# Gathered expert rows for 40 tokens instead of 32, in an encoder block with 16384 product-key experts

## The chip, the core and the metric

The kernel is written by hand in instructions with semaphores and runs on one core of one Trainium2 chip. The metric is the device time of one launch in microseconds (us), as the median of several runs. One core has TensorE (PE; its weight loads are told apart as PEld), VectorE (DVE), ScalarE (ACT), GpSimd (POOL) and SyncE (SP, here only a queue that issues DMAs). "L1014" is line 1014 of the kernel.

## What is computed

One block over 256 tokens of width 2048 (`SEQ`, `D_MODEL`), all in float32. Norm, one large projection, two attention branches, gates, output projection, residual: this part takes the first 700 us and isn't touched. Then comes the expert layer, in the reference:

```python
def peer_ffn(h, w_pq, sub_keys, expert_u, expert_v):
    ...
    q = (t @ w_pq).reshape(n_tok, PEER_HEADS, 2, PEER_QDIM // 2)
    sc = jnp.einsum('thcd,hckd->thck', q, sub_keys, preferred_element_type=jnp.float32)
    top_s, top_i = lax.top_k(sc, PEER_TOPK)
    ...
    best_s, best_j = lax.top_k(cand_s, PEER_TOPK)
    expert_idx = jnp.take_along_axis(cand_i, best_j, axis=-1)
    gate = jax.nn.softmax(best_s, axis=-1)
    ...
        u = expert_u[ib]
        a = jax.nn.gelu(jnp.einsum('thkd,td->thk', u, tb, preferred_element_type=jnp.float32), approximate=False)
        vv = expert_v[ib]
        return jnp.einsum('thk,thkd->td', (gb * a).astype(vv.dtype), vv)
```

Each token picks 8 x 16 = 128 of the 16384 experts. For each it takes the dot of its own 2048 values with the expert's row of `expert_u`, a gelu, a gate, and adds the expert's row of `expert_v` with that weight. A last residual and a norm follow.

## The kernel before

**Two ways to the experts.** The first TD = 224 tokens go through all 16384 experts on TensorE, with a weight that is zero where an expert isn't picked. The last S = 32 tokens fetch only the rows that they picked, by gathers; VectorE multiplies them. S + TD = 256.

**Chunks.** All weights stream in as chunks of 128 x 1024 floats (512 KB), through four buffers (`raw`). ACT rounds a chunk to `hi` (L622), DVE takes the rest `lo` = raw - hi (L1014, two buffers). PE multiplies `hi` with the activations' high and low part side by side ("high" matmul, 2 x TD columns, L1643 in stage "u", L1912 in "down") and `lo` with the high part ("low" matmul, TD columns, L1650 and L1916). A body is four chunks; each has 8 highs and 8 lows. In chunks 0 and 2 of a body the highs come first, in 1 and 3 the lows, so on PE 16 of a kind stand in a row.

**Stage "u"** has 256 chunks (bodies 0 to 63): h times expert_u, gelu, into `act`. In bodies 1 to 21 DVE also finds the picked experts. At body 20 two matmuls with a selection matrix (`sel`, L1872 and L1873) put the picked indices and gates of the last 32 tokens on partitions: four copies (COPIES) of 32 tokens, each copy with another quarter of the 128 picks, so 32 gathers (PICKS) of 128 rows cover the half rows of one table, and STEPS = 64 both halves. In bodies 24 (U0) to 51 (UG - 1) the gates of the dense tokens are **spread** over all experts, four pairs of tokens a body, 112 pairs: POOL writes two `one_j` tiles a pair (L602, four buffers), DVE one `one_i` (L1479, two buffers), PE multiplies them before chunks 0 and 2 of a body, two pairs at a time (L1896, two records each matmul), ACT copies one part of the result (L909), DVE multiplies the other into `act` (L1489). Of each later block DVE multiplies gelu and gate itself (L1499).

**Dots.** POOL issues the gathers (L583) from its own queue, in an order written out with its one_j: the gather of row n + 2 before pair 4n + 2. DVE's dot (L1453) reads the row, which then is free for the next gather but one (two row buffers). `dots_of` (L144) puts one dot after chunk 3 of each body from 22 (UR) to 51, then two a body; the last is in body 4 of "down".

**Stage "down"** has two halves of 128 chunks (32 bodies): act times expert_v, for output columns 0 to 1023 and 1024 to 2047. ACT and DVE make `act_now` (L924, L1531) for each chunk. In the first half, after body WEIGHED = 5, DVE adds the gathered rows of expert_v, weighted, into `acc` (L1563, L1566); `adds_of` (L151) puts one in every 2.75 chunks of the first half, from chunk 28 on, and one in every 3.5 of the second. In the last body of each half PE adds the copies up by a product with `fold` (L1968), after it has waited for all adds of that half.

**Queues.** Each engine runs its instructions in the order in which the kernel gives them. SP's queue holds all loads of weights in order; a load waits until `lo` of the chunk four before is made. Each engine's order in a body is that of its functions: DVE in the spread does lo of the next chunk, one_i, the sum of the block's two halves (`upper`, L1020, chunks 0 and 2), act x gates, act x upper (chunks 1 and 3), and the dot last.

## Time and profile before

| | |
|---|---|
| time, median of 3 runs (range) | 2140.78 us (2140.64 to 2142.12) |
| profiled execution, its time | 2139.2 us |
| its span, first to last instruction | 2137.2 us |
| PE busy | 2108.7 us, 99% |
| DVE busy | 1584.1 us, 74% |
| ACT busy | 1118.9 us, 52% |
| POOL busy | 488.8 us, 23% |
| DMA | 482.26 MB, mean 226 GB/s |

The page counts an engine as busy while an instruction of it runs, and matmuls overlap, so a busy PE is not one at its peak; how fast it goes is read from the starts in the timeline. Shares of busy time are means over stages with different limits. Stage "u" lies between 772.8 and 1469 us, its spread between 1010 and 1345, "down" between 1470 and 2123.

### The profile page before, as it was taken

The numbers are of one execution on the slowest core, as the hardware profiler recorded it, in microseconds if no ns is written. First come the engines' busy times: TensorE is split into PE (matmuls) and PEld (weight loads), VectorE is DVE, ScalarE is ACT, GpSimd is POOL, SyncE is SP. The second block draws the span as 40 slices with busy tenths as digits, with TensorE's granted clock in tenths as the row PEclk, the third lists the DMA queues.
The fourth block names the chain that finished last, engine by engine and source line by source line (L and its number), as shares of the span: only waits on it lengthen the run. The fifth ranks groups of instructions, "written<-read, shape, count | busy, mean of one in ns | idle before, by whom it ended". The sixth has DMA issues, their size and how long they took to land.

```text
span 2137.2 us, 40878 instructions
## 1 busy us (share of the span) xinstructions
PE 2108.7 (99%) x13494; PEld 1973.4 (92%) x13494; DVE 1584.1 (74%) x2622; ACT 1118.9 (52%) x1879; POOL 488.8 (23%) x379
## 2 busy tenths in 40 slices
PE   8999999999999999999999999999999999999997
PEld 6888888889989999999999999999999999999997
DVE  6555566667777986888778888888777776777775
ACT  5444455446455655556555555555555554555553
POOL 0000000000000000001999999332222220111110
PEclk9999999999999999999999999999999999999998
DMA  7655554445556556666767666888877776877773
GB/s 246 235 187 190 183 166 157 149 155 189 181 192 230 166 174 210 207 210 224 228 221 222 222 221 222 286 309 313 312 286 291 285 283 215 267 275 266 268 251 128
DMA packets 134750, 482.26 MB, mean 226 GB/s; under 512 B 15455, under 2 KB 18399, under 8 KB 134295
## 3 DMA queue, kind: packets, MB, share of 16 engines
q1 hardware_dynamic: 116072, 414.29, 57.6%
q0 software_dynamic: 18432, 67.12, 8.8%
q8 instruction: 27, 0.44, 0.1%
q14 instruction: 45, 0.36, 0.1%
q10 hardware_dynamic: 174, 0.05, 0.0%
HBM read 477.16 MB, written 4.24 MB: 225 GB/s over the span
## 4 chain that ended last, share of the span: by engine, by line
PE 95%; DVE 3%; issue 1%; DMA 1%; ACT 0%; DVEq 0%; SPq 0%; ACTq 0%
PE ps L1643 35%; PE ps L1912 19%; PE ps L1650 19%; PE ps L1916 11%; PE ps L1673 5%; PE ps L1896 2%; DVE lo L1014 1%; PE ps L1767 1%; PE ps L1749 1%; PE ps L1758 0%; DMA raw<-w_down 0%; DMA x_t<-x_t 0%; DVE score_b L1322 0%; DVE idx_now L1324 0%; DVE top_now L1328 0%
## 5 line engine op out<-in xcount | busy, mean ns | idle before, releaser
L1014 DVE TENSOR_TENSOR lo<-raw,hi 128x1024 fp32r<-128x1024 f32 x760 | 935.3, 1231 | 473.5 <-PE ps L1643 144.5
L622 ACT CAST hi<-raw 128x1024 fp32r<-128x1024 f32 x760 | 795.7, 1053 | 346.8 <-DMA raw<-w_down 137.6
L1643 PE MATMUL ps<-move_u,hi 128*128 128x448 f32 x2048 | 451.1, 368 | 0.0
L1912 PE MATMUL ps<-act_now,hi 128*128 128x448 f32 x2048 | 439.8, 365 | 0.4 <-ACT hi L622 0.4
L1912 PEld LDWEIGHTS ps<-act_now,hi 128*128 128x128 f32 x2048 | 375.0, 188 | 26.4 <-issue 0.7
L1643 PEld LDWEIGHTS ps<-move_u,hi 128*128 128x128 f32 x2048 | 371.0, 189 | 24.6
L1643 PE MATMUL ps<-move,hi 128*128 128x512 f32 x1536 | 379.3, 395 | 9.5 <-ACT hi L622 9.5
L1643 PEld LDWEIGHTS ps<-move,hi 128*128 128x128 f32 x1536 | 281.5, 189 | 62.9 <-issue 9.5
L630 ACT COPY upper<-ps 128x224 f32<-128x224 f32 (+1 forms) x224 | 80.3, 358 | 484.3 <-PE ps L1643 484.2
L602 POOL TENSOR_SCALAR one_j<-iota,j_t,gate_t 128x128 f32<-128x128 f32 x224 | 296.8, 1331 | 3.0 <-ACT j_t L880 1.8
L1916 PEld LDWEIGHTS ps<-act_now,lo 128*128 128x128 f32 x2048 | 250.6, 191 | 7.3 <-DVE lo L1014 2.0
L1916 PE MATMUL ps<-act_now,lo 128*128 128x224 f32 x2048 | 252.1, 274 | 2.1 <-DVE lo L1014 2.0
L1650 PEld LDWEIGHTS ps<-move_u,lo 128*128 128x128 f32 x2048 | 248.4, 191 | 5.1 <-DVE lo L1014 1.5
L1650 PE MATMUL ps<-move_u,lo 128*128 128x224 f32 x2048 | 249.0, 274 | 1.1 <-DVE lo L1014 1.0
L1650 PEld LDWEIGHTS ps<-move,lo 128*128 128x128 f32 x1536 | 198.1, 191 | 11.2 <-DVE move L1066 1.3
L1650 PE MATMUL ps<-move,lo 128*128 128x256 f32 x1536 | 202.3, 284 | 1.0 <-DVE move L1239 0.9
L583 POOL DMA_INDIRECT rows<-w_down,idx x64 | 93.9, 1467 | 452.5 <-DVE acc L1566 371.7
L583 POOL DMA_INDIRECT rows<-u_rows,idx x64 | 85.8, 1341 | 437.8 <-ACT gates_s L866 318.2
L1531 DVE TENSOR_TENSOR act_now<-act,act_now 128x224 fp32r<-128x224 f32 x256 | 98.8, 386 | 13.3 <-ACT act_now L924 12.9
L1673 PE MATMUL ps<-move,hi 128*128 128x256 f32 x512 | 97.4, 286 | 2.8 <-DVE lo L1014 2.8
L924 ACT CAST act_now<-act 128x224 fp32r (+1 forms) x256 | 95.7, 374 | 0.0
L554 POOL COPY q_now<-qk 128x256 f32 x8 | 4.1, 515 | 363.5 <-DVE qk L1027 207.0
(206 smaller groups left out, 1628.2 us busy)
## 6 DMA issues: line engine op xcount, KB each, us to landing
raw<-w_u SPq DMA_DIRECT2D x256, 512.0 KB
raw<-w_down SPq DMA_DIRECT2D x256, 512.0 KB
raw<-w_qk SPq DMA_DIRECT2D x68, 512.0 KB
raw<-w_gate SPq DMA_DIRECT2D x64, 512.0 KB
raw<-w_out SPq DMA_DIRECT2D x32, 512.0 KB
raw<-w_pq SPq DMA_DIRECT2D x32, 512.0 KB
raw<-w_v SPq DMA_DIRECT2D x28, 512.0 KB
raw<-w_o SPq DMA_DIRECT2D x24, 512.0 KB
```

The source lines that it names most:

```text
L583: nc.gpsimd.indirect_dma_start(rows[n % 2][:], None, lines, bass.IndirectOffsetOnAxis(ap=idx[:, n:n + 1], axis=0)).then_inc(row_landed[n % ...
L602: ins = nc.gpsimd.tensor_scalar(one_j[n % 4][:, t % 2, :], iota128[:], j_t[:, t:t + 1], gate_t[:, t:t + 1], ALU.is_equal, ALU.mult)
L622: nc.scalar.copy(hi[slot][:], raw[slot][:]).then_inc(hi_ready, 1)
L630: nc.scalar.copy(upper[e][:, 0:w], ps[e][:, w:2 * w]).then_inc(upper_ready, 1)
L924: nc.scalar.copy(act_now[s % ACTS][:, 0:TD], pick1(act, j)).then_inc(act_hi_ready, 1)
L1014: nc.vector.tensor_tensor(lo[s % LOS][:], raw[s % RAW][:], hi[s % RAW][:].bitcast(F32), ALU.subtract).then_inc(lo_ready, 1)
L1531: nc.vector.tensor_tensor(act_now[s % ACTS][:, TD:2 * TD], pick1(act, j), act_now[s % ACTS][:, 0:TD].bitcast(F32), ALU.subtract).then_inc( ...
L1643: ins = nc.tensor.matmul(ps[bank][:, 0:2 * w], hi[slot][:, col:col + P], m, start=begins, stop=ends)
L1650: ins = nc.tensor.matmul(ps[bank][:, 0:w], lo[lslot][:, col:col + P], m[:, 0:w], start=False, stop=False, skip_group_check=True)
L1673: ins = nc.tensor.matmul(ps[bank][:, 0:T], w[:, col:col + P], x, start=begins, stop=ends)
L1912: return nc.tensor.matmul(ps[d][:, 0:2 * TD], hi[s % RAW][:, d * P:(d + 1) * P], act_now[s % ACTS][:], start=begins, stop=ends)
L1916: return nc.tensor.matmul(ps[d][:, 0:TD], lo[s % LOS][:, d * P:(d + 1) * P], act_now[s % ACTS][:, 0:TD], start=False, stop=False, skip_gro ...
```

## The change

S becomes 40 and TD 216; 40 tokens in three copies fill 120 partitions (NP). A copy has a third of the picks, so PICKS is 43 in place of 32 and STEPS 86 in place of 64. PAIRS is 108 (was 112) and the spread ends after body 50. There are three row buffers (ROWS) instead of two. DOT_AT, a list, holds the place of each dot: after chunk 3 of every body from 22, after chunk 1 too in the odd bodies 25 to 49 and in all from 51 on; the last is in body 8 of "down" and WEIGHED is 9. In the spread, the gather of a row now stands before the pair two places ahead of its dot. The adds start at chunk 44 of "down" and come every 1.88 chunks in the first half, from chunk 2 of the second every 2.88; the last of each half is at its chunk 123. Gathers of expert_v no longer wait for all dots, only for their own buffer. The selection is six matmuls with three matrices, the indices are copied by two ACT instructions in place of eight. `fold` is loaded before x2, when PE is through with stage "u".

```diff
-S = 32
+S = 40
 TD = T - S
 COPIES = P // S
-PICKS = PH * TOPK // COPIES
+NP = COPIES * S
+PICKS = -(-PH * TOPK // COPIES)
+ROWS = 3
 STEPS = 2 * PICKS
...
+DOT_AT = [it * BODY + s for it in range(UR, (CHUNKS["u"] + CHUNKS["down"]) // BODY) for s in (1, 3)
+          if s == 3 or it >= UG or it > U0 and it % 2 != U0 % 2][:STEPS]
+WEIGHED = DOT_AT[-1] // BODY + 1 - CHUNKS["u"] // BODY
...
+def row_before_pair(n):
+
+    return tuple(g for g in range(2, STEPS) if DOT_AT[g] < UG * BODY and max(0, DOT_AT[g] - U0 * BODY - 2) == n)
...
-    first, apart = (2, 7 / 2) if half else ((WEIGHED + 2) * BODY, 11 / 4)
+    first = 2 if half else (WEIGHED + 2) * BODY
+    apart = (HALF * BODY - 5 - first) / (PICKS - 1)
...
             sp.wait_ge(move_free, 1)
+            sp.dma_start(fold[:], A["fold"]).then_inc(fold_in, 16)
...
-                if table == "u_rows" and n >= 2:
-                    pool.wait_ge(dot_done, n - 1)
-                if table == "w_down":
-                    pool.wait_ge(dot_done, min(STEPS, STEPS - 1 + n))
-                    if n >= 2:
-                        pool.wait_ge(row_added, n - 1)
+                g = n + STEPS * (table == "w_down")
+                if ROWS <= g:
+                    pool.wait_ge(dot_done, min(STEPS, g - ROWS + 1))
+                if ROWS + STEPS <= g:
+                    pool.wait_ge(row_added, g - ROWS - STEPS + 1)
...
             for n in range(PAIRS):
-                if n % BODY == 2:
-                    gather("u_rows", n // BODY + 2)
+                for g in row_before_pair(n):
+                    gather("u_rows", g)
...
-                    for q in range(COPIES):
-                        own = slice(q * S, (q + 1) * S)
-                        nc.scalar.copy(idx[own, :].rearrange("p (c m) -> p c m", c=2),
-                                       ps[7][own, 0:2 * P].rearrange("p (c k) -> p c k", c=2)[:, :, own])
-                        ins = nc.scalar.copy(gates_s[own, :], ps[7][own, 2 * P + q * S:2 * P + (q + 1) * S])
-                    ins.then_inc(idx_ready, 1)
+                    nc.scalar.copy(idx[0:NP, :], ps[7][0:NP, 0:STEPS])
+                    nc.scalar.copy(gates_s[0:NP, :], ps[7][0:NP, 2 * P:2 * P + PICKS]).then_inc(idx_ready, 1)
...
+            for q, own in enumerate(own_of):
+                nc.tensor.matmul(chosen[:, :, 0:own.stop - own.start], sel[:, q, :], e_pair[:, :, own],
+                                 start=q == 0, stop=q == COPIES - 1)
+            for q, own in enumerate(own_of):
+                ins = nc.tensor.matmul(ps[7][0:NP, 2 * P:2 * P + own.stop - own.start], sel[:, q, :], found_g[:, 1, own],
+                                       start=q == 0, stop=q == COPIES - 1)
...
                 pe.wait_ge(row_added, PICKS * (half + 1))
+                pe.wait_ge(fold_in, 16)
```

## Rows read from the trace of the kernel before

**Rows 1.** The page: engines busy, and the chain that ended last by engine.
```profile
PE 2108.7 (99%) x13494; PEld 1973.4 (92%) x13494; DVE 1584.1 (74%) x2622; ACT 1118.9 (52%) x1879; POOL 488.8 (23%) x379
...
PE 95%; DVE 3%; issue 1%; DMA 1%; ACT 0%; DVEq 0%; SPq 0%; ACTq 0%
```
**Rows 2.** Timeline of PE, stage "qk": start us, duration us, instructions.
```profile
102.73 3.82 PE L1643 MATMUL ps<-move,hi 128*128 128x512 f32 x16
106.39 2.08 PE L1650 MATMUL ps<-move,lo 128*128 128x256 f32 x16
108.30 3.82 PE L1643 MATMUL ps<-move,hi 128*128 128x512 f32 x16
```
**Rows 3.** Timeline of PE, stage "u" before the spread.
```profile
902.18 1.94 PE L1650 MATMUL ps<-move_u,lo 128*128 128x224 f32 x16
903.96 3.40 PE L1643 MATMUL ps<-move_u,hi 128*128 128x448 f32 x16
907.20 1.94 PE L1650 MATMUL ps<-move_u,lo 128*128 128x224 f32 x16
```
**Rows 4.** Timeline of PE, the fold matmuls and what follows them.
```profile
1785.22 1.88 PE L1968 MATMUL ps<-fold,acc 128*128 128x32 f32 x16
...
1786.93 1.13 PE L1916 MATMUL ps<-act_now,lo 128*128 128x224 f32 x8
```
**Rows 5.** Timeline of PE in the spread.
```profile
1206.82 1.05 PE L1896 MATMUL ps<-one_j,one_i 128*128 128x128 f32 x8
...
1212.74 1.05 PE L1896 MATMUL ps<-one_j,one_i 128*128 128x128 f32 x8
```
**Rows 6.** Timeline of POOL in the spread.
```profile
1204.00 1.03 POOL L583 DMA_INDIRECT rows<-u_rows,idx  x1 [0.17 <-issue]
1205.07 10.60 POOL L602 TENSOR_SCALAR one_j<-iota,j_t,gate_t 128x128 f32<-128x128 f32 x8
```
**Rows 7.** Line L602: durations ns (least, median, most), idle before them.
```profile
L602 POOL TENSOR_SCALAR one_j<-iota,j_t,gate_t x224: 783/1401/3615, 1009.6 to 1340.3; 128x128 f32<-128x128 f32 x112
...
  ACT j_t L880: 1.8, 1
```
**Rows 8.** Timeline of POOL at the spread's end.
```profile
1335.31 5.73 POOL L602 TENSOR_SCALAR one_j<-iota,j_t,gate_t 128x128 f32<-128x128 f32 x4
```
**Rows 9.** Timeline of all engines there: PE's last spread.
```profile
1342.98 1.05 PE L1896 MATMUL ps<-one_j,one_i 128*128 128x128 f32 x8
```
**Rows 10.** Timeline of POOL, one narrow window: a single one_j.
```profile
1206.56 3.01 POOL L602 TENSOR_SCALAR one_j<-iota,j_t,gate_t 128x128 f32<-128x128 f32 x1
```
**Rows 11.** Timeline of DVE in the same stretch.
```profile
1206.71 1.22 DVE L1453 CUSTOM_DVE_ANT_0 rows<-rows,h_rows 128x1024 f32<-128x1024 f32 x1
...
1208.99 0.42 DVE L1479 TENSOR_TENSOR one_i<-ps,iota 128x256 f32<-128x256 f32 x1
```
**Rows 12.** Stretches of POOL: from:to, us, busy (instructions), PEclk, DMA share, GB/s.
```profile
1027.47:1033.37 5.90, 5.90 (x4) 1.00 0.78 220
1033.38:1038.06 4.68, 4.68 (x4) 1.00 0.66 197
1205.07:1211.12 6.05, 6.05 (x4) 1.00 0.73 212
1211.14:1215.66 4.52, 4.52 (x4) 1.00 0.65 205
```
**Rows 13.** Timeline of POOL late in stage "u".
```profile
1429.92 1.68 POOL L583 DMA_INDIRECT rows<-u_rows,idx  x1 [3.34 <-DVE dots L1453]
```
**Rows 14.** Timeline of DVE late in the spread.
```profile
1322.96 1.33 DVE L1014 TENSOR_TENSOR lo<-raw,hi 128x1024 fp32r<-128x1024 f32 x1 [1.08 <-ACT hi L622]
...
1328.88 1.23 DVE L1014 TENSOR_TENSOR lo<-raw,hi 128x1024 fp32r<-128x1024 f32 x1
```
**Rows 15.** Line L1566: durations ns of the adds.
```profile
L1566 DVE SCALAR_TENSOR_TENSOR acc<-rows,w_s,acc x62: 1276/1279/1280, 1548.2 to 2073.4; 128x1024 f32<-128x1024 f32 x62
```
**Rows 16.** Stretches of all engines: busy PE, PEld, DVE, ACT, POOL, then as above.
```profile
1380.00:1420.16 40.16, 40.16 (x257) 38.33 (x257) 33.24 (x49) 22.27 (x33) 13.41 (x9) 1.00 0.89 318
```

More of the change, by code:

```diff
@@ L366, in build @@
         e_pair = at("e_pair", ARENA + 98 * KB, [P, 2, P])
-        sel = at("sel", ARENA + 99 * KB, [P, P])
-        rows = [at(f"rows{i}", ARENA + (112 + 4 * i) * KB, [P, CW]) for i in range(2)]
+        sel = at("sel", ARENA + 96 * KB, [P, COPIES, NP])
+        rows = [at(f"rows{i}", ARENA + (112, 116, 108)[i] * KB, [P, CW]) for i in range(ROWS)]
         acc = at("acc", ARENA + 120 * KB, [P, D])
         idx = at("idx", MOVE + 31 * KB, [P, STEPS], U32)
-        dots = at("dots", MOVE + 31 * KB + 256, [P, STEPS])
-        gates_s = at("gates_s", MOVE + 31 * KB + 512, [P, PICKS])
-        w_s = at("w_s", MOVE + 31 * KB + 640, [P, PICKS])
-        fold = at("fold", MOVE + 31 * KB + 768, [P, S])
+        dots = at("dots", MOVE + 31 * KB + 352, [P, STEPS])
+        gates_s = at("gates_s", MOVE + 31 * KB + 704, [P, PICKS])
+        w_s = dots[0:NP, 0:PICKS]
+        fold = at("fold", MOVE + 16 * KB + 2 * TD * 4, [P, S])
         x2 = at("x2", MOVE, [P, KT, T])
@@ L606, in _ @@
             nc.gpsimd.memset(ones[:], 1.0).then_inc(ones_ready, 1)
-            for n in range(PAIRS // BODY + 2, STEPS):
-                gather("u_rows", n)
+            for n in range(STEPS):
+                if DOT_AT[n] >= UG * BODY:
+                    gather("u_rows", n)
             for n in range(STEPS):
@@ L1449, in dot_of @@
             def dot_of(n):
-                v.wait_ge(row_landed[n % 2], 16 * (n // 2 + 1))
-                c = n // PICKS * CW
-                nc.vector.tensor_tensor_reduce(rows[n % 2][:], rows[n % 2][:], h_rows[:, c:c + CW], 1.0, 0.0, ALU.mult, ALU.add,
-                                               dots[:, n:n + 1]).then_inc(dot_done, 1)
+                v.wait_ge(row_landed[n % ROWS], 16 * (n // ROWS + 1))
+                c, row = n // PICKS * CW, rows[n % ROWS][0:NP, :]
+                nc.vector.tensor_tensor_reduce(row, row, h_rows[0:NP, c:c + CW], 1.0, 0.0, ALU.mult, ALU.add,
+                                               dots[0:NP, n:n + 1]).then_inc(dot_done, 1)
             def dots_at(it, s):
@@ L1549, in weights_at @@
                     v.wait_ge(dot_done, STEPS)
-                    nc.vector.tensor_tensor(w_s[:], dots[:, 0:PICKS], dots[:, PICKS:STEPS], ALU.add).then_inc(w_summed, 1)
+                    nc.vector.tensor_tensor(w_s, dots[0:NP, 0:PICKS], dots[0:NP, PICKS:STEPS], ALU.add).then_inc(w_summed, 1)
                 if (it, s) == (WEIGHED + 1, 1):
@@ L1870, in _ @@
             pe.wait_ge(e_ready, 1)
-            pe.wait_ge(sel_in, 16 * 2)
-            nc.tensor.matmul(ps[7][:, 0:2 * P], sel[:], e_pair[:].rearrange("p c k -> p (c k)"), start=True, stop=True)
-            nc.tensor.matmul(ps[7][:, 2 * P:3 * P], sel[:], found_g[:, 1, :], start=True, stop=True).then_inc(e_turned, 1)
+            pe.wait_ge(sel_in, 16)
+            own_of = [slice(q * PICKS, min((q + 1) * PICKS, P)) for q in range(COPIES)]
+            chosen = ps[7][0:NP, 0:2 * PICKS].rearrange("p (c m) -> p c m", c=2)
+            for q, own in enumerate(own_of):
[4 more added lines that the diff above has]
+                                       start=q == 0, stop=q == COPIES - 1)
+            ins.then_inc(e_turned, 1)
             with pe.Fori(INDEXED, UR + 1) as it:
@@ L1905, in _ @@
                     body("u", two * 2 + (U0 + k), before=spread_gates(k))
+            for it in range(UG - (UG - U0) % 2, UG):
+                body("u", it, before=spread_gates((it - U0) % 2))
             with pe.Fori(UG, CHUNKS["u"] // BODY) as it:
@@ L1966, in last_body @@
                 pe.wait_ge(row_added, PICKS * (half + 1))
+                pe.wait_ge(fold_in, 16)
                 for d in range(8):
-                    nc.tensor.matmul(ps[d][:, 2 * TD:2 * TD + S], acc[:, (8 * half + d) * P:(8 * half + d + 1) * P], fold[:],
+                    nc.tensor.matmul(ps[d][:, 2 * TD:2 * TD + S], acc[0:NP, (8 * half + d) * P:(8 * half + d + 1) * P], fold[0:NP, :],
                                      start=False, stop=False, skip_group_check=True)
@@ L2038, in columns, with own_copies @@
     return np.ascontiguousarray(b.reshape(-1, P, CW))
+def own_copies():
+    sel = np.zeros((P, COPIES, NP), np.float32)
+    for q in range(COPIES):
+        sel[P - S:, q, q * S:(q + 1) * S] = np.eye(S, dtype=np.float32)
+    return sel
 def weave(wa, wb):
@@ L2061 @@
         "ident": np.eye(P, dtype=np.float32),
-        "sel": np.ascontiguousarray(np.tile(np.eye(P, dtype=np.float32)[:, P - S:], (1, COPIES))),
-        "fold": np.tile(np.eye(S, dtype=np.float32), (COPIES, 1)),
+        "sel": own_copies(),
+        "fold": np.pad(np.tile(np.eye(S, dtype=np.float32), (COPIES, 1)), ((0, P - NP), (0, 0))),
         "bias_rows": bias_rows(),
```

36 lines of the change are left out of this document (17 added, 19 removed).

## The prediction

> **What bounds the kernel now.** I read the page first: PE is busy for 99% of the span and holds 95% of the chain that ended last [rows 1]. So time goes down only if TensorE has less to stream, and goes up wherever another engine makes it wait. What it streams follows from the code: eight "high" matmuls of 448 columns and eight "low" ones of 224 for each of the 512 chunks of the expert layer, 4096 of either kind. The timeline of PE then gives the pitch of each kind, start to start, which the mean duration hides because matmuls overlap: 16 highs of 512 columns take 106.39 - 102.73 = 3.66 us, 16 of 448 take 3.24 us; 16 lows of 256 columns take 1.91 us, of 224 take 1.78 us [rows 2, 3]; 16 matmuls of only 32 columns take 1.71 us [rows 4]. Last I looked at who runs beside PE while the gates are spread (1010 to 1345 us), because there POOL is busy all the time.
>
> **TensorE, what is removed.** TD goes from 224 to 216, so a high has 432 columns. From 512 to 448, 64 columns fewer save 0.42 us per 16, so 16 fewer save 0.105 us; 4096/16 = 256 such groups give 26.9 us. All of it lies on the path, as PE is it. For the lows (224 to 216) I take nothing: the pitch at 224 columns is 111 ns and at 32 columns still 107 ns, so what sets it is no longer columns. The bounds are 0 and, by the slope between 256 and 224 columns (0.13 us per 16 for 32), 0.13/4 x 256 = 8.3 us.
>
> Here a rule of the Trainium skill speaks for more: "TensorE: Matmul & The Clock Gate", section "Back-to-back issue gap", has an isolated gap of N/2.4 + 2.5 ns, by which 4096 lows would give 4096 x 8/2.4 ns = 13.7 us more (an estimate from that page). The trace contradicts it at these widths, with 107 ns at 32 columns, and the page itself says that the formula undercounts at small N.
>
> **Smaller parts on PE.** There are 108 pairs of tokens to spread in place of 112. Two pairs (8 records) lengthen a half body from 5.02 us [rows 3] to 5.92 us [rows 5], so a pair costs 0.45 us: 1.8 us saved. Picking the gathered indices takes six matmuls in place of two; a float32 matmul leaves two records, as those of the spread do, so it is eight records more at some 0.11 us: 0.9 us lost. The fold matmuls have 40 columns in place of 32, at the same floor [rows 4]: nothing. **Without any new wait PE saves 26.9 + 1.8 - 0.9 = 27.8 us.**
>
> **POOL in the spread, where a wait is added.** This is the part that decides. For each pair POOL writes two one_j tiles, and a body holds four pairs. In steady state its timeline is one gather (1.03 us), gaps of 0.17 and 0.04 us, and eight one_j in 10.60 us: 11.84 us, which is exactly twice PE's 5.92 [rows 5, 6]. It never waits for a buffer to come free: the only idle time before any of the 224 one_j is 1.8 us at the very start, and none of them waits for a matmul of the spread [rows 7]. An engine with time to spare would run ahead to its four buffers and wait there. This one stays about 2 us ahead of its need to the end: the last one_j ends at 1341.04, the last two pairs are multiplied from 1342.98, the second of them 0.45 us later, 2.4 us after [rows 8, 9]. So POOL has no surplus.
>
> Why it is so slow: a one_j takes 783 ns when free and up to 3615 [rows 7]. The one of 1206.56 takes 3.01 us: meanwhile DVE runs the dot (from 1206.71) and the next lo, both with two inputs in SBUF, and it ends 0.58 us after that lo has given way to one_i at 1208.99, which has one input in PSUM [rows 10, 11]. So a dot on DVE costs POOL time, too. Four one_j in a half with a dot take 5.90 us early and 6.05 in the middle; in a half without, 4.68 and 4.52 [rows 12]. The difference is 1.22 to 1.53 us, about one dot (1.22 us [rows 11]).
>
> The Trainium skill has the rule behind this ("SBUF — State Buffer", section "Who interferes with whom"): a DVE instruction with two SBUF inputs contends with a GpSimd instruction that reads SBUF, and the second to come blocks. The trace agrees. It speaks against this change.
>
> The change puts three gathers and three dots where two bodies had two of each, and it does so 13 times (bodies 25 to 49). Per two bodies POOL gets 1.03 + 0.17 + 0.04 = 1.24 us more of gather and 1.22 to 1.53 of waiting, and the time that PE leaves it shrinks by 4 x 0.105 = 0.42 us. In full that is 2.88 to 3.19 us. If the gather falls into a wait that POOL has anyway it costs nothing: 1.22 + 0.42 = 1.64 us. The new gathers stand between the two pairs of a half, mostly after the long wait and not in it, but a late POOL shifts them; gathers of the later stage wait themselves (1.68 us in place of 1.03) [rows 13]. Below 1.64 only a finer interlocking of the two engines could bring it: the end is 0. I take a third of the gather, 2.05 us: 13 x 2.05 = 26.7 us, less the 2.4 us of lead that POOL has once: **24.3 us**. Queued behind POOL are only its own one_j and gathers; PE waits for the one_j at the spread's matmuls, and everything else waits for PE.
>
> **DVE.** A half body with a dot is full late in the spread: lo at 1322.96, the next released lo at 1328.88, no idle, 5.92 us; the half without ends with 1.08 us idle [rows 14]. In 5.82 us a half with a dot overruns by at most 0.10, three in a row by 0.3, and the fourth gives back over 1. DVE makes a lo while PE is still in the chunk before, which hides it: nothing; without that cover it would be 39 x 0.1 = 3.9 us. In "u" after body 51 a pair of chunks has one dot as now. In "down" the dots go on to body 8 in place of 4 and the adds come every 1.88 chunks in place of 2.75 and every 2.88 in place of 3.5. An add is 1.28 us [rows 15]: per 4.91 us DVE has two lo (2.46 [rows 14]), two act_now (some 0.8, estimated from the 0.42 of one_i over 256 columns [rows 11]) and 1.06 adds (1.36), together 4.62. It fits; the five places where adds follow in neighbouring chunks overrun for one pair: 0 to 2 us, I take 0.
>
> **DMA.** A gather moves 0.49 MB. With a chunk (0.524 MB) every 2.46 us, the dot phase has the same 313 GB/s as now, and the adds of the first half 213 + 106 = 320 GB/s. Now 318 GB/s, at a DMA share of 0.89, leave PE without a gap (40.16 us busy of 40.16) [rows 16]. Cost 0, and up to 3 us if 320 is just too much. SP issues one small load (fold) more before x2, while four chunks are in flight: nothing. The last add is at chunk 123 of 128, PE asks for it after chunk 124, 2.5 us later; its cover is thin but it happens only twice: 0 to 2 us, I take 0. Three row buffers give each gather one more dot of time to land; PE waits for no row now, so nothing is gained. The eight small ACT copies that become two are beside PE.
>
> **The sum.** The profiled execution took 2139.2 us, 1.6 below the median of 2140.78. From the median: 2140.8 - 27.8 + 24.3 = **2137 us**.
>
> **The rivals.** (a) POOL interlocks with DVE as well with three dots as with two, and the columns are gained in full: 2140.8 - 27.8 = 2113, with small remains 2110 to 2122. For it: the lead of 2.4 us has been constant, so the present rate is a locked one and need not be the highest. Against it: no time is left over and the demand grows by a tenth. 24%. (b) The lows shrink with their columns after all, by the slope between 256 and 224: 8 us less than the forecast, 2129, or 2105 together with (a). Against it: the 107 ns at 32 columns. 6%. (c) Slower: the new gather falls outside the waits each time, so that POOL is short by the full 2.88 to 3.19 us per two bodies; 13 times that less 2.4 is 35 to 39 us, and the time 2148 to 2152. It decides from (27.8 + 2.4)/13 = 2.32 us per two bodies on; from 2.65 on it can be measured. For it: order of the gathers. 14%. (d) That the change doesn't do what it says: DVE or DMA hold up the down stage by 3 to 5 us; inside the range of the forecast.
>
> **How the numbers follow.** The forecast has 56%, and its own range is 2131 to 2145 (1.64 us to some 2.7 per two bodies). A measurement here tells about 0.2% (4.3 us) from no change: faster means below 2136.5, slower above 2145. Of the forecast's 56, 24 lie below, 30 within, 2 above. With (a) and (b) faster has 54%, within 30%, slower 2 + 14 = 16%. The range takes in (a) and reaches to the beginning of (c): 2110 to 2149; what it leaves out is most of (c) and what is worse.
>
> **What would show it.** Right: PE at 432 columns has 16 highs in about 3.14 us and 16 lows still in 1.78; POOL busy without a gap from the first to the last one_j; the spread's matmuls wait for one_j, mostly in odd bodies; 27 bodies of the spread take more than 27 x 11.63 = 314 us, some 338. Under (a) they take 314 and no wait for POOL is in the list. Under (b) the lows have a pitch of 109 ns. Wrong in kind: idle time of PE in the dot or add phases, with DMA or DVE as its releaser.

## The result, and the profile after

The changed kernel takes 2200.56 us (median of 4 runs, 2195.37 to 2206.2), the kernel before 2141.45 beside it (2140.64 to 2145.96): ratio 1.0272, 95% interval 1.0242 to 1.0302. It is slower by 59 us where 4 us less were forecast, and lies above the whole range. The profiled run took 2199.36 us, with a span of 2197.6. Ratios here and below are those of executions side by side, so they differ a little from the quotients of the medians, and one slow execution of e1 (2288.26 us at a mean granted clock of 0.849, where its nine others have 0.993 to 0.996) is left out of its ratio.

From the page of the changed kernel: PE's row, the DMA share in 40 slices, the two big DMA queues (packets, MB, share of 16 engines), the chain by engine and by line.

```profile
PE 2109.4 (96%) x13486; PEld 1986.5 (90%) x13486; DVE 1635.3 (74%) x2680; ACT 1114.6 (51%) x1867; POOL 532.9 (24%) x415
...
DMA  7655554445556567668777778999999998999994
...
DMA packets 141087, 499.84 MB, mean 227 GB/s; under 512 B 17534, under 2 KB 20478, under 8 KB 140630
...
q1 hardware_dynamic: 116072, 414.41, 59.0%
q0 software_dynamic: 24768, 84.56, 15.0%
...
PE 61%; DMA 13%; POOL 13%; DVE 7%; issue 3%; ACT 1%; SPq 0%; DVEq 0%; ACTq 0%; POOLq 0%
```

Before, PE held 95% of the chain and DMA 1% [rows 1]; now 61%, with DMA and POOL at 13% each. From the kernel before, the same two queues, and one stretch of 100 us (busy PE, PEld, DVE, ACT, POOL, then granted clock, DMA share, GB/s):

```profile
q1 hardware_dynamic: 116072, 414.29, 57.6%
q0 software_dynamic: 18432, 67.12, 8.8%
...
1500.00:1600.00 100.00, 100.00 (x637) 95.33 (x636) 75.84 (x102) 54.93 (x84) 20.11 (x13) 1.00 0.83 300
```

q0 carries the gathered rows. Its bytes grew by a quarter, its share of the engines by 70%. The number that decides this case is the engine time of one gathered row, small packets included: share x span x 16 / rows. Before it is 0.088 x 2137.2 x 16 / (128 gathers x 128 rows) = 184 ns, after it is 0.150 x 2197.6 x 16 / (172 x 120) = 256 ns.

Where the time went is read from the starts of the matmuls in PE's timeline: first matmul of "u", first and last of the spread, first, middle and last "high" of down (us), in the profiled execution of each kernel. e1 and e5 are two of the experiments below. "PE alone" marks the shortest that any kernel here with 432 columns had.

```
stage                before   changed   e1     e5     PE alone
u before the spread  244.6    240.5     240.6  240.5  240.5
spread               326.4    336.4     332.3  322.1  309.2
u after it           126.1    147.5     133.7  133.4  133.4
down, first half     325.5    359.9     321.6  321.1  321.1
down, second half    327.4    325.0     326.6  325.3  323.8
span                 2137.2   2197.6    2144.0 2131.1
```

The spread grew as forecast, though it has one body less (27 for 28; that body now counts in the stage after it, which at PE's own pace would take 133.4 us for 126.1). Over "PE alone" the two stages behind the spread are 14.1 and 38.8 us too long, and for those the forecast had nothing. Stretches of the changed kernel there, with the same columns:

```profile
1400.00:1470.00 70.00, 64.00 (x392) 60.14 (x391) 50.66 (x74) 31.80 (x48) 17.25 (x13) 0.98 1.02 282
1500.00:1600.00 100.00, 91.49 (x562) 87.08 (x563) 73.61 (x108) 47.32 (x74) 27.84 (x18) 0.97 1.02 294
1700.00:1830.00 130.00, 117.22 (x745) 111.67 (x743) 97.98 (x117) 59.69 (x92) 32.82 (x24) 1.00 1.02 280
```

The DMA engines are full (1.02) and move only 282, 294 and 280 GB/s; before they moved 318 at 0.89 [rows 16]. Before, PE was busy in all of the 100 us from 1500, with 300 GB/s at 0.83. The waits of the changed kernel name the same, and POOL's one_j in the spread (us in total, times, longest):

```profile
ACT hi L631 <- DMA raw<-w_down: 309.0, 191, 5.1
...
ACT hi L631 <- DMA raw<-w_u: 60.4, 45, 2.8
...
PE ps L1932 <- DVE lo L1019: 30.7, 33, 2.5
...
PE ps L1910 <- POOL one_j L610: 17.8, 9, 3.4
```

The chunk (raw) lands late, ACT's hi and DVE's lo with it, and PE waits for lo: the list shows DVE, the cause is one step further back, at the DMA. PE's wait is the one that counts: before, it was 2.0 us at this place and not 30.7. ACT's wait for raw alone tells little, as it is 276.8 us in e1 below too, where PE waits for lo 4.0 us.

Some of PE's stalls cost more than themselves, as the granted clock falls with them. Before, it was 1.00 in every stage from the spread to the end of down; here it is 0.98 over the spread, and 0.97 or 0.98 in two of the stretches above. One case in the spread, from PE's timeline, and the stretch from 1040.3 us (busy PE, PEld, DVE, ACT, POOL, then as above):

```profile
1041.30 1.22 PE L1910 MATMUL ps<-one_j,one_i 128*128 128x128 f32 x4 [3.04 <-POOL one_j L610]
1042.16 3.23 PE L1650 MATMUL ps<-move_u,hi 128*128 128x432 f32 x8
1045.19 2.87 PE L1657 MATMUL ps<-move_u,lo 128*128 128x216 f32 x16
1047.89 1.75 PE L1650 MATMUL ps<-move_u,hi 128*128 128x432 f32 x8
...
1040.30:1047.10 6.80, 5.80 (x22) 5.57 (x22) 0.32 (x2) 1.73 (x4) 6.49 (x8) 0.50 0.68 183
```

PE waits 3.04 us, and from 1040.3 to 1047.1 us the granted clock is 0.50 (1.2 GHz): eight highs then take 3.03 us and the sixteen lows 2.70, where they take 1.66 and 1.77 at 1.00. A share of 0.98 over 336 us means some 13 us at that level, an estimate, so up to some 6 of the spread's 27 us over "PE alone" are the clock. The forecast had no such term.

PE's own pitch at the full clock is what was forecast, in its timeline:

```profile
1604.97 3.31 PE L1928 MATMUL ps<-act_now,hi 128*128 128x432 f32 x16
1608.12 1.94 PE L1932 MATMUL ps<-act_now,lo 128*128 128x216 f32 x16
1609.89 2.32 PE L1928 MATMUL ps<-act_now,hi 128*128 128x432 f32 x11
```

Sixteen highs take 1608.12 - 1604.97 = 3.15 us (3.24 at 448 columns), sixteen lows 1609.89 - 1608.12 = 1.77 [rows 3].

### The profile page after: what moved, and what is told of

Read it like the earlier page. It is cut to its first block, busy times and chain, and to the rows that moved or that the text cites. A ratio compares the mean times of both kernels' runs of the same rounds, so it can differ in the third digit from the quotient of the medians.

```text
span 2197.6 us, 40971 instructions
## 1 busy us (share of the span) xinstructions
PE 2109.4 (96%) x13486; PEld 1986.5 (90%) x13486; DVE 1635.3 (74%) x2680; ACT 1114.6 (51%) x1867; POOL 532.9 (24%) x415
## 4 chain that ended last, share of the span: by engine, by line
PE 61%; DMA 13%; POOL 13%; DVE 7%; issue 3%; ACT 1%; SPq 0%; DVEq 0%; ACTq 0%; POOLq 0%
PE ps L1650 24%; PE ps L1657 13%; POOL one_j L610 11%; PE ps L1928 11%; DMA raw<-w_down 9%; PE ps L1932 6%; PE ps L1680 5%; DVE lo L1019 4%; DMA raw<-w_u 4%; POOL rows L591 2%; PE ps L1756 1%; PE ps L1774 1%; ACT hi L631 1%; DMA raw<-w_o 0%; PE ps L1765 0%
## 5 line engine op out<-in xcount | busy, mean ns | idle before, releaser
L1650 PE MATMUL ps<-move_u,hi 128*128 128x432 f32 x2048 | 442.8, 364 | 0.1
L1928 PE MATMUL ps<-act_now,hi 128*128 128x432 f32 x2048 | 433.6, 362 | 3.8 <-DVE act_now L1536 1.6
L639 ACT COPY upper<-ps 128x216 f32<-128x216 f32 (+1 forms) x224 | 79.1, 353 | 460.4 <-PE ps L1650 458.7
L1932 PE MATMUL ps<-act_now,lo 128*128 128x216 f32 x2048 | 258.2, 275 | 30.7 <-DVE lo L1019 30.7
L1657 PE MATMUL ps<-move_u,lo 128*128 128x216 f32 x2048 | 255.2, 277 | 9.6 <-DVE lo L1019 9.5
L591 POOL DMA_INDIRECT rows<-u_rows,idx x86 | 119.4, 1388 | 491.8 <-ACT gates_s L872 313.8
L591 POOL DMA_INDIRECT rows<-w_down,idx x86 | 123.4, 1435 | 438.2 <-DVE acc L1573 372.5
L1536 DVE TENSOR_TENSOR act_now<-act,act_now 128x216 fp32r<-128x216 f32 x256 | 96.9, 379 | 90.3 <-ACT act_now L929 88.1
L1573 DVE SCALAR_TENSOR_TENSOR acc<-rows,dots,acc 120x1024 f32<-120x1024 f32 x84 | 107.4, 1279 | 0.0
L1458 DVE CUSTOM_DVE_ANT_0 rows<-rows,h_rows 120x1024 f32<-120x1024 f32 x86 | 105.3, 1225 | 0.0
```

The lines of the kernel that those rows point to most:

```text
L591: nc.gpsimd.indirect_dma_start(rows[g % ROWS][0:NP, :], None, lines, bass.IndirectOffsetOnAxis(ap=idx[0:NP, n:n + 1], axis=0)).then_inc(ro ...
L1458: nc.vector.tensor_tensor_reduce(row, row, h_rows[0:NP, c:c + CW], 1.0, 0.0, ALU.mult, ALU.add, dots[0:NP, n:n + 1]).then_inc(dot_done, 1)
L1536: nc.vector.tensor_tensor(act_now[s % ACTS][:, TD:2 * TD], pick1(act, j), act_now[s % ACTS][:, 0:TD].bitcast(F32), ALU.subtract).then_inc( ...
L1573: nc.vector.scalar_tensor_tensor(out=own, in0=row, scalar=w_s[:, m:m + 1], in1=own, op0=ALU.mult, op1=ALU.add).then_inc(row_added, 1)
L1650: ins = nc.tensor.matmul(ps[bank][:, 0:2 * w], hi[slot][:, col:col + P], m, start=begins, stop=ends)
L1657: ins = nc.tensor.matmul(ps[bank][:, 0:w], lo[lslot][:, col:col + P], m[:, 0:w], start=False, stop=False, skip_group_check=True)
```

## The experiments

My theory after the result: 120 rows in one gather are dear for the DMA, whatever the amount. Rival: it is the amount, a quarter more rows in the densest stretch. Four kernels separate them.

**e1: 128 rows, the rest as changed.** The index tile, the gather and `sel` get all 128 partitions, the last eight with rows that nobody reads.

```diff
+GP = P
...
-                nc.gpsimd.indirect_dma_start(rows[g % ROWS][0:NP, :], None, lines,
-                                             bass.IndirectOffsetOnAxis(ap=idx[0:NP, n:n + 1], axis=0)
+                nc.gpsimd.indirect_dma_start(rows[g % ROWS][0:GP, :], None, lines,
+                                             bass.IndirectOffsetOnAxis(ap=idx[0:GP, n:n + 1], axis=0)
```

> The changed kernel, but each gather fetches 128 rows: the selection has 128 columns in place of 120, so the eight added partitions get index 0 and fetch a row that nobody uses. Theory A (a gather of 120 rows is split badly over the DMA engines: after shows 253 ns per gathered 4 KB against 182, and 24 small packets per gather against 16): packets fall back to 16 small ones per gather and some 185 ns per row although 6.7% more bytes move; the DMA share in the dot and add phases falls from 1.0 to about 0.9, PE's gaps there go, and the time falls from 2200 by 50 to 62 us to 2138 to 2150. What remains above 2114 is POOL's part. Rival B (what saturates is the amount: 86 x 2 gathers with three buffers): 6.7% more bytes make it slower or leave it as it is, 2195 to 2215.

Measured: 2147.15 us, ratio 1.0018 (1.0007 to 1.0029). Its two queues, and two stretches:

```profile
q1 hardware_dynamic: 116072, 414.42, 58.3%
q0 software_dynamic: 24768, 90.19, 11.8%
...
1400.00:1470.00 70.00, 70.00 (x456) 68.29 (x455) 58.56 (x86) 39.47 (x57) 24.25 (x14) 1.00 0.91 324
1500.00:1600.00 100.00, 98.82 (x640) 96.03 (x639) 79.44 (x115) 53.39 (x83) 27.70 (x17) 1.00 0.89 315
```

More bytes in the same number of packets, and 0.118 x 2144.0 x 16 / (172 x 128) = 184 ns per row, as before the change. 1.0272 - 1.0018 = 0.0254, or 54 us (some 7 either way by the two intervals): that is the price of 120 rows. It takes in what they do to the weights, whose packets are as many and as large in both kernels and took 0.583 x 2144.0 = 1250 us of each engine here, but 0.590 x 2197.6 = 1297 beside the gathers of 120 rows. Amount as the cause falls: 324 GB/s pass with PE busy all the time.

**e2 and e3: the kernel before with 120 and 112 rows** per gather (the results of the last 8 and 16 partitions are left out). The edit of the gather for 120 rows is shown; dots and adds are narrowed in the same way.

```diff
-                nc.gpsimd.indirect_dma_start(rows[n % 2][:], None, lines,
-                                             bass.IndirectOffsetOnAxis(ap=idx[:, n:n + 1], axis=0)
+                nc.gpsimd.indirect_dma_start(rows[n % 2][0:120, :], None, lines,
+                                             bass.IndirectOffsetOnAxis(ap=idx[0:120, n:n + 1], axis=0)
```

> The kernel before (32 tokens, two row buffers), but gathers, dots and adds run over 120 of the 128 partitions; the results of eight partitions (tokens 24 to 31 of the last copy) are left out. Fewer bytes move than before. Theory A: gathered rows take about 255 ns in place of 182, 24 small packets per gather, the DMA share at 1400 to 1450 us rises from 0.9 to about 1.0 and the kernel becomes slower than before by 5 to 30 us. Rival B (amount): 0 to 2 us faster or unchanged.

> The same with 112 rows, of which the results of 16 partitions are left out. If what matters is that the number of rows divides by 16 (16 x 7), it is like before: 16 small packets per gather, about 180 ns a row, time within 3 us of before. If anything but 128 is slow, the rows take about 255 ns and it is slower by 5 to 30 us as with 120.

Measured: 2162.31 us with 120 rows (1.0089, 1.0069 to 1.0109), 2146.06 with 112 (1.0021, 1.0007 to 1.0035). In e2, with one stretch, then e3:

```profile
DMA packets 134750, 478.07 MB, mean 222 GB/s; under 512 B 16479, under 2 KB 19423, under 8 KB 134295
...
q0 software_dynamic: 18432, 62.93, 11.1%
...
1400.00:1470.00 70.00, 63.53 (x378) 58.76 (x379) 50.10 (x74) 33.33 (x48) 20.93 (x13) 0.98 0.98 267
```
```profile
q0 software_dynamic: 16384, 58.73, 8.8%
```

120 rows cost 19 us even in the old kernel, with less to move; from 1400 to 1470 us PE is busy for 63.53 us in place of 69.64, with the DMA at 0.98. A row takes 249 ns there, 210 ns at 112, where the kernel loses 4.5 us (1.5 to 7.5). The packets show how a gather is made up: 18432 / 128 = 144 = 120 rows + 24 small packets; at 112 rows 128 = 112 + 16.

**e4: the changed kernel without second dots in the spread**, so 13 gathers more fall behind it.

```diff
-          if s == 3 or it >= UG or it > U0 and it % 2 != U0 % 2][:STEPS]
+          if s == 3 or it >= UG][:STEPS]
```

> The changed kernel without the second dot in odd bodies of the spread: DOT_AT has those 13 dots and gathers later, so the dots end some 6 bodies later in down and the adds of the first half come closer together. My theory of POOL: its stalls in the spread (27 us of excess against 53 half bodies of 5.82 us) go to 0 to 5 us. The 13 gathers move into the phases in which DMA is full, where each costs its transfer, some 1.5 to 2 us: 20 to 26 us lost there. Sum 2190 to 2205. Rival: if the spread is as long as before without the second dot (337 us from its first to its last matmul), POOL isn't stalled by dot and gather but by something else.

Measured: 2219.48 us (1.0356, 1.0331 to 1.0380). The spread is 309.2 us, which is 53 half bodies of 5.82 us and 0.8 for the last pairs, and no wait for one_j is left: with one dot per body POOL costs nothing even at 432 columns. But the first half of down grows from 359.9 to 398.6:

```profile
1700.00:1830.00 130.00, 100.79 (x572) 93.67 (x573) 87.57 (x100) 47.55 (x72) 42.17 (x30) 0.92 1.03 256
```

27 us won where POOL was the limit were lost, and 16 more, where the DMA is: 43 us in all, where I had expected to lose 20 to 26. Part of it is the clock, 0.92 in the stretch shown. So the second dots are right in kind; what is left of them in e1, 23.1 us of spread, is POOL's price.

**e5 and e6: POOL's price, two ways down**, both with 128 rows. e5 issues each gather of the spread one pair earlier, between the halves of a body and not between the two pairs whose one_j one half waits for. e6 puts the second dot in every fourth body.

```diff
-    return tuple(g for g in range(2, STEPS) if DOT_AT[g] < UG * BODY and max(0, DOT_AT[g] - U0 * BODY - 2) == n)
+    return tuple(g for g in range(2, STEPS) if DOT_AT[g] < UG * BODY and max(0, DOT_AT[g] - U0 * BODY - 3) == n)
```
```diff
-          if s == 3 or it >= UG or it > U0 and it % 2 != U0 % 2][:STEPS]
+          if s == 3 or it >= UG or it > U0 and it % 4 == (U0 + 1) % 4][:STEPS]
```

> The changed kernel with gathers of 128 rows, and each row gather of the spread issued one pair earlier, so that GpSimd does it between the two halves of a body and not between the two pairs whose one_j one half waits for. If the order inside the body is what makes GpSimd hold TensorE back in the spread (332.3 us from its first to its last matmul with 128 rows, floor 309.3), a good part of the 23 us goes: spread 315 to 325, time 2132 to 2140. If GpSimd's work per body is simply too long (8 one_j of 1.30, two gathers and the time it is blocked by dots against 11.64 us of TensorE), the order changes nothing: spread 332, time 2147.

> The changed kernel with gathers of 128 rows and the second dot of the spread in every fourth body in place of every second, so half of the 13 extra dots and gathers move out of the spread into the last stretch of u and the first of down. By GpSimd's price per extra gather and dot the spread comes down from 332.3 us by half of its 23 us excess, to about 321. Theory: with gathers of 128 rows the DMA has room late, so the last stretch of u and the first half of down lengthen by no more than 3 us and the time is 2134 to 2140, below both kernels. Rival: the DMA takes it back as it did without any second dots (152.3 and 398.6 us with 120 rows): then these two stretches lengthen by over 10 us and the time is 2145 to 2160.

Measured: e5 2133.72 us, ratio 0.9964 (0.9949 to 0.9980); e6 2134.73, ratio 0.9964 (0.9953 to 0.9976). Both beat both kernels, the one before by 0.4%, which is little but outside the intervals. Spread 322.1 and 320.6 us, first half of down 321.1 and 325.2. Why the order helps is to be seen in POOL's own rows; durations (least, median, most) of the gathers and the one_j from 1020 to 1320 us, and PE's wait for one_j in the whole run, first e1, then e5:

```profile
L592 POOL DMA_INDIRECT rows<-u_rows,idx x36: 1026/1027/2098, 1022.5 to 1318.5; - x36
...
L611 POOL TENSOR_SCALAR one_j<-iota,j_t,gate_t x191: 780/944/3002, 1020.0 to 1319.6; 128x128 f32<-128x128 f32 x191
...
PE ps L1911 <- POOL one_j L611: 15.1, 11, 3.0
```
```profile
L592 POOL DMA_INDIRECT rows<-u_rows,idx x37: 1026/1632/2097, 1020.1 to 1311.3; - x37
...
L611 POOL TENSOR_SCALAR one_j<-iota,j_t,gate_t x198: 780/874/2978, 1021.1 to 1317.8; 128x128 f32<-128x128 f32 x198
...
PE ps L1911 <- POOL one_j L611: 7.4, 10, 2.3
```

In e1 most gathers take their free 1.03 us and stand beside the time that POOL is held up by DVE; in e5 the median gather takes 1.63 us, it stands in that time, and the one_j get shorter (944 to 874 ns). The same work fits into 10.2 us less. PE's waits for one_j are 7.7 us of that. The rest is about what the clock took in e1, which has two stretches of 3.4 us at a granted clock of 0.50, each with a stall of over 2 us (from 1040.7 and 1115.8 us); e5 has none in its spread.

**e7 and e8, again as e13 and e14: what holds POOL up.** No second dots, 128 rows, and in every second body four idle adds of 256 columns on VectorE that nobody reads. The twins differ in one operand:

```diff
-nc.vector.tensor_tensor(ps[6][0:NP, 0:T], h_rows[0:NP, 0:T], h_rows[0:NP, T:2 * T], ALU.add)
+nc.vector.tensor_tensor(ps[6][0:NP, 0:T], h_rows[0:NP, 0:T], ps[6][0:NP, 0:T], ALU.add)
```

> The changed kernel with gathers of 128 rows and without second dots in the spread, and in every second body of the spread four idle VectorE adds of 256 columns, both inputs from SBUF, result to a PSUM bank that nobody reads; no further gather. Together they last about as long as one dot (some 1.2 us). If VectorE reading two SBUF inputs is what stops GpSimd, spread (309.2 us without second dots) grows by some 13 x 0.5 to 13 x 1.2 = 6 to 15 us, and one_j beside these adds takes over 2 us. If the extra gather alone is what costs GpSimd's time, it stays at 309 to 311.

> The same with one change: the second input of the four idle adds comes from the PSUM bank and not from SBUF. VectorE is as long busy. If it is the pair of SBUF inputs that stops GpSimd, spread stays at 309 to 311 us here and grows in the kernel beside it; if any VectorE work of this length does it (by its own queue reaching the one_i or gated products later), both grow alike.

> The kernel with four idle adds of two SBUF inputs in every second body of the spread again, timed in rounds beside its twin. If two SBUF inputs stop GpSimd, its spread is 5 to 8 us longer than the twin's again (315.8 against 309.7 in the first look) and its time 0.2 to 0.4% above the twin's. If the first look was scatter, both have the same time within 0.1% and spreads of 309 to 313.

> The twin, the second input of the idle adds from PSUM: spread 309 to 311 us, time about 2137, under both theories; it is the yardstick for the kernel beside it.

Measured: spread 315.8 us with two SBUF inputs and 309.7 with one, the same to a tenth in both pairs of runs. Times 2145.09 and 2137.0 us for e7 and e8 (one execution each), 2146.3 (1.0023, 1.0014 to 1.0033) and 2141.86 (0.9998, 0.9988 to 1.0008) for e13 and e14 (ten each). DVE's row and PE's only wait for one_j in e7, then DVE's row in e8, where PE never waits for one_j:

```profile
L1532 DVE TENSOR_TENSOR ps<-h_rows 120x256 f32<-120x256 f32 x52 | 26.4, 507 | 1.3
...
PE ps L1916 <- POOL one_j L611: 2.5, 1, 2.5
```
```profile
L1532 DVE TENSOR_TENSOR ps<-h_rows,ps 120x256 f32<-120x256 f32 x52 | 22.2, 426 | 1.3
```

22.2 us of VectorE work cost the spread 0.5 us when one input is in PSUM; with both in SBUF it is 6.6. That isn't an even price for each of the 13 groups: 4.3 us fall in one half body (from 1131.6 us in e7), where PE waits 2.5 us for a one_j and then runs 3.4 us at a granted clock of 0.50; four smaller ones give the rest. So it is the pair of SBUF inputs that holds POOL up, and not VectorE's time as such. The Trainium skill says so ("SBUF — State Buffer", section "Who interferes with whom": such an instruction contends with a GpSimd instruction that reads SBUF), and these runs agree: one_j, which reads SBUF, has a median of 1030 ns in e7 and of 968 in e8. The adds themselves are longer, too, 507 ns against 426; part of that may be the operand's place, part POOL holding them up, which isn't separated here.

**e9: both edits of e5 and e6.**

> The changed kernel with gathers of 128 rows, each gather of the spread one pair earlier, and the second dot in every fourth body: the two edits that each gave some 12 us over the kernel with 128 rows alone. If they act on different parts (the order on what one gather costs TensorE, the number on how many there are), spread falls to 314 to 316 us (320.6 and 322.1 with one of them), the first half of down stays at the 325 us of the quarter, and the time is 2127 to 2131. If both only take away the same excess, spread stays at 319 to 321 and with the 4 us more in down the time is 2133 to 2136.

Measured: 2134.99 us (0.9970, 0.9953 to 0.9986), spread 316.6, first half of down 325.6, second 327.9. The spread came within 0.6 us of what the first theory said (314 to 316); down took back 4.5 and 2.6 us against e5, and the time is that of the second theory. The sum of the two is no better than either, and the spread is no longer the place to look.

**e10: two row buffers**, the changed kernel otherwise as it is.

```diff
-ROWS = 3
+ROWS = 2
```

> The changed kernel as it is (gathers of 120 rows, a second dot in every other body) with two row buffers in place of three, 4 KB less of SBUF. A gather then waits for the dot before the last and not for the one before that. If the third buffer matters, GpSimd waits for dots inside the spread with one_j queued behind and spread is 340 us or more (336.4 with three); if the two dots of a body are far enough apart, it is within 2 us of 336.4. In the down half, where DMA sets the pace, the third buffer lets one more gather be in flight; I expect at most 5 us of difference, time 2195 to 2210.

Measured: 2278.27 us (1.0634, 1.0612 to 1.0655), far outside both expectations. The spread takes 404.6 us. Gathers from 1020 to 1400 us, what POOL waited for before them, and their landing:

```profile
L591 POOL DMA_INDIRECT rows<-u_rows,idx x37: 1047/1752/1758, 1026.6 to 1394.8; - x37
...
  DVE dots L1458: 117.6, 25
...
DMA to landing us min/median/max: 5.7/6.8/8.5
```

With two buffers a gather is issued only when the dot before the last is done, and it then takes 6.8 us to land; two dots stand one half body (5.82 us) apart. Gather, landing and dot become one chain, and POOL waits in it with one_j queued behind: PE's wait for one_j is 60.0 us in place of 17.8. The clock adds to it, with a granted mean of 0.89 over this spread, against 0.98 with three buffers; at 404.6 us that is some 85 us at 1.2 GHz in place of some 13, an estimate. The third buffer is what lets the second dot go at this rate: I had it down as gaining nothing, from a kernel with one dot per body.

**e11, e12, e16, e17: the count of rows**, the kernel before with 124, 96, 104 and 64 rows, each the edit of e2 with another number; the results of the partitions above are left out.

> The kernel before with gathers of 124 rows, the results of the last 4 partitions left out. If the cost comes from the count of rows not being a multiple of 16, a gathered row takes about 250 ns of an engine as at 120 (182 at 128, 208 at 112), the queue of the gathers shows 11 to 12% of 16 engines in place of 8.8%, the small packets per gather rise above 16 (31, if the rows go in groups of the largest divisor up to 8), and the time is 2155 to 2165. If it is only fewer rows that make a gather less even, it stays at 9% and 2142 to 2146.

> The kernel before with gathers of 96 rows, the results of the last 32 partitions left out. 96 is 16 times 6: by the rule that a multiple of 16 goes in 16 equal groups, 16 small packets per gather (2048 in all from this queue), about 180 to 210 ns per row, and the queue's share 6.6 to 8%, time 2140 to 2144. If any count under 128 costs more per row, the share is over 8.8% in spite of a quarter fewer rows.

> The kernel before with gathers of 104 rows, the results of the last 24 partitions left out. If the rows go to the largest number of engines up to 16 that divides them, that is 13 with 8 rows each, and the three others get 8 small packets each: 16 + 24 = 40 small packets per gather, 128 x 24 = 3072 more under 512 B than the kernel before, 18527. If the smaller share of engines is what makes a row dear (249 ns at 120 rows on 15 engines, 289 at 124 on 4), it takes 230 to 290 ns here, the queue's share is 9 to 11%, and the time 2142 to 2156. If groups of rows by another rule were behind it, the small packets are another number.

> The kernel before with gathers of 64 rows, the results of the upper 64 partitions left out. 64 rows go to 16 engines with 4 rows each: 16 small packets per gather, 15454 or 15455 under 512 B. At 128 rows (8 for each engine) a row took 184 ns of an engine, at 112 and 96 (7 and 6) 210. If a share of fewer than 8 rows is what makes these dearer, 64 rows take 205 to 230 ns each, share 4.9 to 5.5%; if it was scatter, 185 and 4.4%. Time 2139 to 2144 either way.

Measured, one execution each: 2455.34, 2145.35, 2158.81 and 2142.18 us. The queue of 124 rows with its small packets, the queue of 96, then 104 with its packets, and 64:

```profile
DMA packets 181853, 480.35 MB, mean 196 GB/s; under 512 B 63070, under 2 KB 66014, under 8 KB 181398
...
q0 software_dynamic: 65536, 65.21, 11.7%
```
```profile
q0 software_dynamic: 14336, 50.34, 7.5%
```
```profile
DMA packets 134749, 469.68 MB, mean 218 GB/s; under 512 B 18526, under 2 KB 21470, under 8 KB 134294
...
q0 software_dynamic: 18432, 54.55, 9.4%
```
```profile
q0 software_dynamic: 10240, 33.56, 5.0%
```

All together, with the largest divisor of the count up to 16, the rows for each of that many engines, and the time of the kernel (us; the second row is e1, the others are the kernel before):

```
rows  divisor <= 16  rows each  small packets     ns per row  time
128   16             8          16                184         2141
128   16             8          16                184         2147 (e1)
120   15             8          24 = 16 + 1 x 8   249         2162
112   16             7          16                210         2146
104   13             8          40 = 16 + 3 x 8   244         2159
96    16             6          16                209         2145
64    16             4          16                209         2142
124   4              31         388 = 16 + 12x31  289         2455
```

The small packets follow one rule in all seven counts, and 104 rows were forecast by it before they ran (18527, read 18526): the counts are those of rows that go to the largest number of engines up to 16 that divides them, with as many small packets for each engine left out as the others have rows. The trace doesn't name the engine of a packet, so the engines are inferred from the counts. 104 rows move 13% less than 120 and cost about the same (18 us, one execution), 112 cost 4.5; 96 (3 us) and 64 (2 us), one execution each, lie within the scatter of the kernel before (2138 to 2146). So it is not how many rows there are, but, by this reading of the counts, on how many engines they go. Of the 313 us that 124 rows cost, part is the clock, 0.956 in the mean; a gather of 124 rows takes 15.2 us from issue to landing (median), one of 96 rows 5.9. The Trainium skill has the divisor ("DMA: Bandwidth & Descriptors", section "Why a DMA increments its semaphore by 16 and not by 1": the largest k up to 16 that divides the dimension). The packet counts agree with it. That section of the Trainium skill gives no price for k of 15: by its rule alone each engine has 8 rows at 120 as at 128. The small packets' own time isn't what makes these rows dearer: in the packet records of e2 they take 14 ns each (9 before), 2.7 us of each engine in all, while the 4 KB packets of the gathers went from 182 to 247 ns in the mean and from 159 to 249 in the median. Why a row's own packet takes longer no run separates, the uneven share of the engines being the likely cause; nor why shares of 7, 6 and 4 rows take 209 ns where 8 take 184. The DMA share at 124 rows is only 0.72 from 1400 to 1500 us, where PE is busy for 70% of the time; a few full engines in a mean over 16 would show so, which is argued and not shown.

**e15: the order of e5 with 120 rows left.**

> The changed kernel with its 120-row gathers, each gather of the spread one pair earlier; nothing else. If order and row count are independent, spread falls from 336.4 by the 10 us that the same edit gave with 128 rows, to about 326, the rest stays at 147 and 360 us, and the time is 2187 to 2192. If the slow 120-row gathers are what the early issue meets, rows land later and the gain is smaller: over 2194.

Measured: 2201.78 us (1.0266, 1.0228 to 1.0303), no change against the changed kernel. In the profiled execution, the slowest of the four (2190.08 to 2211.45), the spread fell by 11.3 us to 325.1, as with 128 rows; the stages behind it grew by 2.2, 11.6 and 10.0. The step "and the rest stays" was wrong: here the time won ahead of a stage that the DMA limits (share 1.02) was only waited for there. In e5, with the DMA at 0.90 behind the spread, it was kept.

## Why the prediction was wrong

**The failed step is the term of the DMA: "Cost 0, and up to 3 us if 320 is just too much."** It priced a gather by its bytes, 0.49 MB, and allowed 3 us. The amount was right, and at most the 8 us of down below can be laid to it (e1). The price per row was not: 256 ns in place of the 184 that 128 rows had shown all along. With 172 gathers of 120 rows that is 172 x 120 x 72 ns / 16 = 93 us of all 16 engines, in a kernel whose DMA stood at 0.89 in the densest stretch [rows 16]. The cost was 54 us, 18 times the bound. With the 8 us of down (below) that is the whole of the miss: 2137 + 54 + 8 = 2199. Nothing in the trace of before showed a gather of another count, so the bound from both sides should have been wide; and a rule that I didn't weigh speaks against 120. By the Trainium skill ("DMA: Bandwidth & Descriptors", section "Why a DMA increments its semaphore by 16 and not by 1") 120 rows leave an engine out.

**PE, right.** Highs at 3.15 us (forecast "about 3.14"), lows 1.77, so they don't shrink with their columns; rival (b) is out. A pair of chunks takes 4.92 us in place of 5.02, which is 25.6 us in 256 pairs (forecast 26.9).

**POOL, right in kind, and in size with some luck.** Forecast 24.3 us; the spread of e1 is 332.3 - 309.2 = 23.1 us longer than PE alone needs, of the changed kernel 27.2. Per two bodies, with the 2.4 us of lead, (23.1 + 2.4)/13 = 1.96 us, forecast 2.05. The whole spread was to take "some 338" us and took 336.4. But the third of a gather was a choice between bounds, and the measured sums hold the clock's loss, which was no term: e1's two stretches at 0.50, 6.8 us together, are up to 3.4 us of its 23.1. The 1.64 for a gather that falls into a wait can be undercut by "a finer interlocking", as the prediction allowed: e5 has (12.9 + 2.4)/13 = 1.18. Rivals (a) and (c) are out for this order: PE waits for one_j, and the price isn't the full one.

**DVE and the end of down, small miss.** With 128 rows the sum would be 2137 and e1 measured 2145 (1.0018 x 2141.45). From the first to the last high of down the trace has 652.9 us before and 648.2 in e1. By the pitches (5.02 and 4.92 us for 127.5 pairs of chunks) 12.7 us should have gone, and 4.7 went: the 8 us short are about the whole difference. In the lists of e1 this is small waits of PE and PEld for lo and issue, and ACT's wait for the chunks of w_down, 276.8 us in place of 137.6; that the adds and dots now fill DVE and DMA there more evenly is the likely cause, but that is only argued. I had 0 for it, and 3 to 5 as rival (d).

**The buffers, half right.** By three buffers "nothing is gained": against the changed kernel with two, 78 us are.

**Chances.** Slower had 16%, all of it for POOL. No part of it stood for the resource at 0.89, where a small rise of the price per row suffices.

## What to carry to other kernels

Count the rows of an indirect gather as engines get them, not as bytes: keep a multiple of 16, best 128, and pad with rows nobody reads (e1: 54 us back by moving 6.7% more). When the DMA is full in the stage behind (1.02), time won ahead of it is lost again (e4, e15); at 0.90 it was kept (e5). So unload the full resource first, and allow in the forecast for the clock that a stalled PE loses. A GpSimd instruction that issues DMAs is best placed where DVE's two-SBUF dots would hold GpSimd up anyway (e5: 10 us by moving each call by one pair, some 3 of them from the clock).

## What was not expected of the hardware

- A gathered row of 4 KB costs 184 ns of a DMA engine with 128 rows per gather, 209 to 210 with 112, 96 or 64, 249 with 120, 244 with 104, 289 with 124, small packets included; 124 rows make the same kernel 15% slower, the fall of the granted clock to 0.956 included.
- A full DMA (share 1.02) moves 280 to 294 GB/s with such gathers, where 324 pass with 128 rows at a share of 0.91.
- GpSimd's issue of a gather takes 1.03 us or up to 2.1 in the spread. The long ones lie beside a dot and the next lo on DVE, so the time that DVE holds it up seems to be inside it, and such an instruction can serve as filler; e5 agrees, no run isolates it.
- With a stall of PE of 2.3 to 3 us the granted clock fell to 0.50 for 3.4 or 6.8 us (changed kernel, e1, e7), so that a wait for POOL can cost more than its length; not every such wait did this, the longest of e5, 2.3 us, had no fall.
